# A PEER expert layer at the end of a one-core trunk step: rows of the second stream gathered as 64 tokens with two picks each, query low parts on GpSimd, four pieces of the choice inside the projection

## The reference, cut to what matters

```python
q = (h @ w_q).reshape(b, l, PEER_HEADS, 2, PEER_KEY_DIM // 2)
s = jnp.einsum('blhpk,hpnk->blhpn', q, sub_keys).astype(jnp.float32)
sv, si = lax.top_k(s, kk)
cand = sv[..., 0, :, None] + sv[..., 1, None, :]
cv, ci = lax.top_k(cand.reshape(b, l, PEER_HEADS, kk * kk), kk)
...
expert = i1 * PEER_N_KEYS + i2
gate = jax.nn.softmax(cv, axis=-1).astype(h.dtype)
...
act = jax.nn.gelu(jnp.einsum('tkd,td->tk', u[ex], hx), approximate=False)
return jnp.einsum('tk,tkd->td', gx * act, v[ex])
```

## Time and profile before

| | |
|---|---|
| median of 3 runs | 3093.76 us (3091.87 to 3102.01) |
| the profiled execution | 3091.47 us, its span 3089.4 us |
| TensorE | busy 75% of the span |
| VectorE | 72% |
| ScalarE | 40% |
| GpSimd | 38% |
| DMA | 866.75 MB, mean 281 GB/s |
| mean granted TensorE clock | 0.862 of full |

### The profile page before, as it was taken

The page is one execution under the profiler, slowest core; times in us unless marked ns, Lnnn a source line. Parts: engine busy times, 40 slices in busy tenths (PEclk is TensorE's granted clock), DMA queues, the critical chain, the costliest instruction groups (busy, mean ns, idle before and its releaser), DMA issues.

```text
span 3089.4 us, 38793 instructions
## 1 busy us (share of the span) xinstructions
PE 2319.5 (75%) x15046; PEld 2046.4 (66%) x15046; DVE 2235.4 (72%) x2892; ACT 1229.6 (40%) x1951; POOL 1168.7 (38%) x793
## 2 busy tenths in 40 slices
PE   6899999999999899999998930000331048999997
PEld 2688889988887798999987930000231047888886
DVE  1344446878888863444545899999999988999985
ACT  1233334545555563433343410000893065444433
POOL 0000000255455530000000022686888846767760
PEclk8899999999999999999999975555555568999998
DMA  9888775544534459876553567999999967999994
GB/s 407 329 305 294 288 289 202 190 141 164 178 137 150 157 199 379 307 265 236 177 204 136 178 282 250 362 421 422 422 421 422 422 225 268 375 376 377 360 365 141
DMA packets 151913, 866.75 MB, mean 281 GB/s; under 512 B 18177, under 2 KB 30481, under 8 KB 74017
## 3 DMA queue, kind: packets, MB, share of 16 engines
q1 hardware_dynamic: 67698, 447.32, 39.4%
q0 software_dynamic: 73872, 406.08, 34.2%
q10 hardware_dynamic: 10160, 10.88, 1.0%
HBM read 836.81 MB, written 27.39 MB: 280 GB/s over the span
## 4 chain that ended last, share of the span: by engine, by line
PE 51%; DVE 15%; POOL 14%; issue 9%; DMA 8%; ACT 2%; DVEq 0%; ACTq 0%; SPq 0%; POOLq 0%
PE bank L1693 30%; POOL u_ring L686 14%; PE bank L2060 7%; PE bank L1679 7%; DMA raw<-in_tiles 4%; DVE w_lo L1109 3%; DMA v_got<-in_v_rest,expert 2%; PE bank L1718 2%; DVE u_ring L1572 2%; DVE peer_g L1600 2%; PE bank L2043 2%; DMA u_ring<-in_peer_u,expert 1%; DVE conv L1223 1%; DVE c_lo L1612 1%; DVE y_w L1281 1%
## 5 line engine op out<-in xcount | busy, mean ns | idle before, releaser
L1109 DVE TENSOR_TENSOR w_lo<-raw,w_hi 128x1024 fp32r<-128x1024 f32 x482 | 638.6, 1339 | 559.9 <-ACT w_hi L729 553.6
L729 ACT ACTIVATE w_hi<-raw 128x1024 fp32r<-128x1024 f32 x482 | 501.1, 1058 | 640.9 <-PE bank L1693 340.3
L686 POOL DMA_INDIRECT u_ring<-in_peer_u,expert x256 | 481.3, 1880 | 409.5 <-PE bank L1693 212.8
L1693 PE MATMUL bank<-h_lo,w_hi 128*128 128x256 f32 x2048 | 592.4, 289 | 14.3 <-DVE h_lo L1155 8.3
L1572 DVE CUSTOM_DVE_ANT_0 u_ring<-u_ring,h_t 128x2048 f32<-128x2048 f32 x256 | 580.2, 2289 | 28.1 <-DMA u_ring<-in_peer_u,expert 26.6
L1693 PE MATMUL bank<-h_hi,w_lo 128*128 128x256 f32 x2048 | 581.5, 284 | 0.0
L1693 PE MATMUL bank<-h_hi,w_hi 128*128 128x256 f32 x2048 | 581.4, 284 | 0.0
L1693 PEld LDWEIGHTS bank<-h_lo,w_hi 128*128 128x128 f32 x2048 | 394.8, 193 | 57.0 <-issue 24.6
L693 POOL DMA_INDIRECT v_got<-in_v_rest,expert x256 | 346.0, 1351 | 183.0 <-DVE peer_g L1600 135.8
L1693 PEld LDWEIGHTS bank<-h_hi,w_lo 128*128 128x128 f32 x2048 | 395.0, 193 | 0.9
L1693 PEld LDWEIGHTS bank<-h_hi,w_hi 128*128 128x128 f32 x2048 | 394.6, 193 | 0.0
(11 more groups left out here) (304 smaller groups left out, 4553.8 us busy)
## 6 DMA issues: line engine op xcount, KB each, us to landing
raw<-in_tiles SPq DMA_DIRECT2D x337, 1024.0 KB, 5.7
v_raw<-in_v_dense SPq DMA_DIRECT2D x128, 660.0 KB, 7.1
s_t<-in_states POOLq DMA_DIRECT2D x8, 512.0 KB, 7.1
y_hi_rows<-y_hi_e POOLq DMA_DIRECT2D x16, 256.0 KB, 2.4
y_lo_rows<-y_lo_e POOLq DMA_DIRECT2D x16, 256.0 KB, 6.2
gate_rows<-gate_buf ACTq DMA_DIRECT2D x8, 512.0 KB, 6.6
y_hi<-y_hi_rows POOLq DMA_DIRECT2D x8, 512.0 KB, 8.3
y_lo<-y_lo_rows POOLq DMA_DIRECT2D x8, 512.0 KB, 4.2
```

What stands on the lines that cost most here:

```text
L686: pool.indirect_dma_start(u_ring[:, U_SLOT[e]], None, a["peer_u"][0], bass.IndirectOffsetOnAxis(ap=expert[:, s, k:k + 1], axis=0)).then_in ...
L729: act.activation(w_hi[:, i % RING], raw[:, slot % SLOTS, (n % 2) * 2 * CH:(n % 2 + 1) * 2 * CH], ACT.Copy) \
L1109: dve.tensor_tensor(w_lo[:, i % RING], raw[:, n // 2 % SLOTS, (n % 2) * 2 * CH:(n % 2 + 1) * 2 * CH], w_hi[:, i % RING].bitcast(F32), ALU. ...
L1693: ins = pe.matmul(spot if x.shape[1] == KT else spot.rearrange("p (s t) -> p s t", s=NS), w[:, col], moving, start=start and k == 0 and m ...
```

## The change

It has four parts.

1. `w_lo` of the 32 halves of the query projection is made by GpSimd (a new semaphore `lo_wq`), no longer by VectorE; both copies of `peer_q` out of PSUM are ScalarE's.
2. The order of the choices is (0,0), (1,0), (0,1), (1,1) in the projection, with nothing in between, then (0,2), (0,3), (1,2), (1,3), with the products of u rows in between.
3. The 128 gathers of stream 1 take other rows: the first 64 bring the picks of tokens 0 to 63 (partitions 0 to 63 hold pick k, 64 to 127 pick k + 64), the last 64 those of tokens 64 to 127. For this SyncE's queue copies `expert`, `gate_t` and `h2_t` into arranged tiles (`expert1`, `gate1`, `h2_late`). After the first 64, their tokens are scattered (16 batches, ScalarE alone makes the one-hot tiles) beside the last 64 gathers.
4. After the last u row, 16 batches are left. ScalarE makes `hot_b` of the even ones, VectorE that of the odd ones (one 128x512 comparison) and all `hot_a`; one v add for every second batch (8), the split of blocks 0 and 1 inside it. The last 64 gathers use a ring of 7 slots; two `v_raw` tiles and two `v_got` tiles lie in slots of that ring, and are filled once those are done with.

```diff
+U_LATE = (16, 17, 18, 12, 13, 14, 15)
...
+CHOICES = [(0, 0), (1, 0), (0, 1), (1, 1), (0, 2), (0, 3), (1, 2), (1, 3)]
...
+            sp.dma_start(h2_late[low], h2_t[high, 1]).then_inc(expert1_in, 16)
+            sp.dma_start(h2_late[high], h2_t[high, 1]).then_inc(expert1_in, 16)
+            for of in (low, high):
+                for to in (low, high):
+                    sp.dma_start(expert1[to, of], expert[of, 1, to]).then_inc(expert1_in, 16)
+            sp.wait_ge(expert1_in, 16 * 6)
+            sp.dma_start(h2_t[high, 1], h2_t[low, 1]).then_inc(gate1_in, 16)
...
             for i in range(N_KEYS):
+                if 0 < i < TABLE:
+                    sp.wait_ge(u_used, max(U_DEAD[17], U_DEAD[18]) + 1)
...
+            for i in range(WQ_NO, len(SPLIT)):
+                n = SPLIT[i]
+                pool.wait_ge(hi_done, i + 1)
+                pool.wait_ge(split_used, SPLIT[i - RING] + 1)
+                pool.tensor_tensor(w_lo[:, i % RING], raw[:, n // 2 % SLOTS, (n % 2) * 2 * CH:(n % 2 + 1) * 2 * CH],
+                                   w_hi[:, i % RING].bitcast(F32), ALU.subtract).then_inc(lo_wq, 1)
...
-            for j in range(4):
-                advance_to(min(FIRST["wq", j] + HALVES + LEAD + 3, N_HALVES + LEAD))
-                limit = min(FIRST["wq", j] + 2 * HALVES + LEAD, N_HALVES + LEAD)
-                choose(0, j, lambda: next_half(limit))
+            while at_half[0] < N_HALVES + LEAD:
+                advance()
+            for s, j in CHOICES[0:4]:
+                choose(s, j, lambda: None)
...
+            one_hot(0, 0)
+            for b in range(BATCHES):
+                if b + 1 < BATCHES:
+                    one_hot(0, b + 1)
+                scatter_copy(0, b)
+                if b == BATCHES - 5:
+                    gelu_of_half(0)
...
+            for b in range(HALF_B, BATCHES):
+                if b % 2 and b + 1 < BATCHES:
+                    one_hot(1, b + 1)
+                scatter_copy(1, b)
+                if b in (HALF_B + 6, HALF_B + 10):
+                    dense_hi((b - HALF_B - 6) // 4)
```

More of the change, by code:

```diff
@@ L46 @@
 BATCHES = P // BATCH
+HALF_T = P // 2
+HALF_B = BATCHES // 2
 NEG = -1.0e30
@@ L126 @@
 U_SLOT, U_TURN, U_LAST = ring_slots()
+U_DEAD = {n: max(e for e in range(NS * SEL) if U_SLOT[e] == n) for n in U_LATE}
 def accumulators():
@@ L433, in program @@
         x2_saved = sem("x2_saved")
-        u_in = [sem(f"u_in{n}") for n in range(2 * U_RING)]
+        u_in = [sem(f"u_in{n}") for n in range(2 * U_RING + 3)]
+        expert1_in = sem("expert1_in")
+        gate1_in = sem("gate1_in")
         u_used = sem("u_used")
@@ L1102, in split @@
             def split(n):
-                if n not in SPLIT_NO:
+                if n not in SPLIT_NO or SPLIT_NO[n] >= WQ_NO:
                     return
@@ L1570, in expert_act @@
                 dve.wait_ge(u_in[U_SLOT[e]], 16 * U_TURN[e] + 16)
-                u = u_ring[:, U_SLOT[e]]
-                dve.tensor_tensor_reduce(out=u, in0=u, in1=h2_t[:, s], scale=1.0, scalar=0.0,
-                                         op0=ALU.mult, op1=ALU.add, accum_out=act_p[:, s, k:k + 1]).then_inc(u_used, 1)
-            def coefficients(s):
-                dve.wait_ge(gelu_done, s + 1)
-                dve.tensor_tensor(coef_p[:, s], act_p[:, s], gate_t[:, s], ALU.mult).then_inc(coef_ready, 1)
+                u = u_ring[U_SLOT[e]]
@@ new lines, in expert_act, with coefficients @@
+                h = h2_t[:, s]
+                if e == SEL:
+                    dve.wait_ge(gate1_in, 16 * 5)
+                if e >= SEL + HALF_T:
+                    h = h2_late[:]
+                dve.tensor_tensor_reduce(out=u, in0=u, in1=h, scale=1.0, scalar=0.0,
+                                         op0=ALU.mult, op1=ALU.add, accum_out=act_p[:, s, k:k + 1]).then_inc(u_used, 1)
+            def coefficients():
+                dve.wait_ge(gelu_done, 1)
+                dve.tensor_tensor(coef_p[:, 0], act_p[:, 0], gate_t[:, 0], ALU.mult).then_inc(coef_ready, 1)
@@ L1619, in take @@
                 taken[0] += 1
-            for j in range(4):
-                choose(1, j, take)
+            for s, j in CHOICES[4:]:
+                choose(s, j, take)
             normalise(0)
             normalise(1)
+            dve.sem_inc(gate_max, 1)
             for e in range(taken[0], SEL):
                 expert_act(e)
-            coefficients(0)
+            coefficients()
             for k in range(SEL):
+                if k == HALF_T + 13:
+                    half_coefficients(0)
                 expert_act(SEL + k)
-            coefficients(1)
-            for i in range(2):
-                dense_lo(i)
-            for b in range(BATCHES):
+            half_coefficients(1)
+            e = 0
+            for b in range(HALF_B, BATCHES):
                 one_hots(b)
-                expert_add(b)
-            e = BATCHES
+                if b % 2 == 0:
+                    expert_add(e)
+                    e += 1
+                if b in (HALF_B + 7, HALF_B + 11):
+                    dense_lo((b - HALF_B - 7) // 4)
             for i in range(N_KEYS):
@@ L2047, in _ @@
             pe.wait_ge(score_in, 4)
-            for s in range(NS):
-                turn_picks(s)
-                for b in range(BATCHES):
-                    scatter(s, b)
+            turn_picks()
+            turn_keys()
+            for b in range(BATCHES):
+                scatter(0, b)
+            turn_coef(0)
+            for b in range(HALF_B):
+                scatter(1, b)
+            turn_coef(1)
+            turn_back()
+            for b in range(HALF_B, BATCHES):
+                scatter(1, b)
+            pe.wait_ge(pick_ready, 5)
             pe.wait_ge(scat_copied, NS * BATCHES)
```

223 lines of the change are left out of this document (146 added, 77 removed).

## The result

The changed kernel takes 3067.4 us (median of 4 runs, 3064.08 to 3069.75), the kernel before 3094.49 us beside it. The ratio is 0.991, with a 95% interval of 0.9896 to 0.9924: faster by 27 us, clear of the noise though under 1%, where 41 to 44 us were forecast, and 1.4 us outside the forecast range (3036 to 3066). A repetition (the fifth experiment) gave 3065.0 us, 0.9903 [0.9885, 0.992]. One of the ten runs of e1 took 10333.66 us and is left out of its ratio.

The account below looks back on a forecast made before the run. Bounds: TensorE in the projection, VectorE then DMA in the gathers; in the scatter ScalarE was busy 77 of 82 us. Terms -8 + 3.8 + 0 - 39.9 + 3.4 = -40.7 us from 3091.47 gave 3050.8, predicted 3050, range 3036 to 3066.

Parts of the forecast that it names:

- What bounds, and the scatter: Stream 1's scatter: first half hides beside gathers with 41 us over; stage after last row 42.7 against 82.6 us, -39.9.
- 4.3 us a pair: After the last u row: each of 8 pairs of scatter batches was taken at 4.3 us, 34.4 in all.
- 1.3 us a split: After the last u row: two splits of a v block inside the chain, 2 x 1.3 us.
- Low parts on GpSimd, and the four choices: Query projection: subtractions on GpSimd cost 0; choices slowed 18 us by waiting, first product at 1813 us, gain 8 us.
- The copies of `h2_t` ... at 417 GB/s cost 3.8 us: Gather stage: three 64x2048 copies, 1.57 MB, add 3.8 us of DMA time in a saturated stretch; bounds 0 and 3.8.
- Two move to the last five rows; same bytes, so 0: Gather stage: two of three first `v_raw` loads move to the last five rows, at cost 0.
- The v side: 124 blocks carry adds, not 112: 12 x (3.88 - 3.60) = +3.4 us, bounds 0 and 6.
- The rivals: Five alternatives: late choices (0.17), everything hides (0.14), late pairs no faster (0.05), GpSimd binds projection (0.04), first-half scatter late (0.02).
- The late choices: Rival: GpSimd and VectorE hold each other up, first product at 1821 us or later; 3058 to 3065 us, chance 0.17.
- the ring of 7: Last 64 gathers: one slot less (7 for 8) leaves 15 us for a gather to land; cost taken as 0.

Follow-up runs that it names:

- the fifth experiment: The changed kernel run again unaltered, beside three variants on one chip: 3065.03 us, 0.9903.
- e1: The kernel before with only GpSimd's low parts and the new order of choices (parts 1 and 2): 3088.85 us against 3094.3, 0.9982.
- e12: e6 with VectorE's split of v blocks 0 and 1 one batch later in its queue: 3051.87 us, 0.9851.
- e2: The changed kernel with GpSimd subtracting only 8 of 1024 columns of each projection half, waits kept: 3055.7 us, 0.9884.
- e3: The changed kernel with the three copies of `h2_t` issued when `h2_t` is complete, not after the last choice: 3056.11 us, 0.9875.
- e6: The changed kernel with the edits of e3 and e4 together: 3051.24 us, 0.9863.
- e7: As e6, but the copies of `h2_t` wait for the fifth choice: 3051.3 us, 0.9869.
- e8: The changed kernel with one extra 128-partition copy of `h2_t` (1.05 MB) ahead of the others: 3066.7 us in one run.
- e11: The changed kernel with the eight 16 KB copies of `expert` and `gate_t` made twice: 3068.01 us in one run.
- e4: The changed kernel with the loads of v blocks 1 and 2 issued after the last product of a u row: 3062.13 us, 0.9895.
- e10: The changed kernel without the gathers of v rows 5 to 255, all 256 adds kept: 3047.83 us in one run.

## Why the prediction was off

**What bounds, and the scatter: right.** The early half of the scatter hid with 43 us to spare (41 worked out), and the stage after the last row is 42.0 us (42.7). Inside it the terms were off, 3.68 for 4.3 us a pair and 2.9 and 3.4 for 1.3 us a split; that the sum fits within 0.8 us is luck. The split is dear because it is a chain over two engines: ScalarE's 1.29 us, then VectorE's 1.53, then the hot tile queued behind. e12 shows it.

**Low parts on GpSimd, and the four choices: mechanism right, size near.** TensorE stayed the bound of the projection (102.73 of 103 us, e1), and the two engines held each other up by 20 us, forecast 18; with the 0.8 us from the last choice to the product and chance, the first product came 3.9 to 6.7 us earlier, not 8. e2 shows that the mutual waiting is all of it. The Trainium skill, "SBUF — State Buffer", section "Who interferes with whom", also says that the reduction never contends and that a cast can; the trace agrees in both, with 0.69 us always and once 2.32 us for a 128x32 cast (0.18 alone).

**"The copies of `h2_t` ... at 417 GB/s cost 3.8 us": the step that failed.** I priced bytes at the rate of 128-partition transfers; the term of +3.8 us, called an upper end, measured +7.6. The three copies touch 64 partitions each, and while they run the rate is 250 GB/s at full DMA share. Product 121 lost 7.6 us although two v loads (3.2 us) had left the stretch, so the gross cost is near 11 us by my estimate; the 7.8 us that the engines lost from 1952.5 to 1980 us and the 3.8 of the copies' own bytes make 11.6. e3 takes 7.1 us back by moving them. The early copies are not free either: from product 1 to 253 e3, e6 and e7 still lose 1.4 to 2.0 us, with the two v loads gone, where e1, without copies and with all its v loads, loses 0.4. e8 and e11 exclude copies within SBUF as such, and small pieces. That 64 partitions are the reason is what these two leave, and the two rows under e8 show it in the rate: 0.52 against 0.86 MB in 2.5 us. The crossing from one half of the partitions to the other wasn't tested apart from it. The Trainium skill, "SBUF — State Buffer", section "Door 1: The DMA port swizzle (why `[64,N]` ≈ `[32,N]`)", says that partitions 0 to 63 reach only half of the DMA's ports, and so do 64 to 127. By this rule 1.57 MB cost 7.5 us at half of 417 GB/s, an estimate from that page's rule and this trace's rate. The 7.1 us that e3 takes back lie nearer to it than to my 3.8; the gross estimate of 11 us lies over both, and no run tells what the copies take from what the gathers beside them lose.

**"Two move to the last five rows; same bytes, so 0": right as a sum, wrong as a place.** The 3.2 us left the stretch near 1955 us and came back as 3.3 us of waits in the last three rows. But in the new place they need not have been paid, with idle DMA engines (share 0.39) right behind; e4 has them there for nothing.

**The v side: wrong by 5.8 us, half understood.** I had 12 x 0.28 us for 12 more blocks with adds. e10 shows that VectorE's 3.75 us, not TensorE's 3.60, is the floor of such a block and that the gathers of v rows cost time on top. With this v side eight of the eleven kernels took 516.5 to 520.2 us, 1 to 5 more than the 515.4 of the kernel before, around the 3.4 that I had forecast. But e1, whose v side is that of the kernel before, took 518.5, so these few microseconds are not told apart from chance. The changed kernel, its repetition and e11 took 524.6, 524.0 and 522.5, with the same code behind the first matmul. Waits of VectorE in this part, changed kernel, then e3:

```profile
DVE peer_g L1690 <- DMA v_got<-in_v_rest,expert: 22.9, 28, 2.5
```

```profile
DVE peer_g L1690 <- DMA v_got<-in_v_rest,expert: 17.1, 23, 2.5
```

Five more waits for a v row, 5.8 us. Why these kernels have them and the others not stays open.

**The rivals.** The late choices (3058 to 3065 us) were the nearest case by number, but not by cause: in the changed kernel the choices cost 3 us of the 18 that were missing in the profiled execution, the copies and v loads 7, the v side 6, the mark 2, and 1 lies between products 121 and 253, where e6 and e7 lose 1.5 and 2.1; whether the ring of 7 has a part in it no run shows. The scatter gave 1 back. No forecast case had the copies as its mechanism, though their bound of 3.8 us was called an upper end.

## What to carry to other kernels

Price a DMA by its bytes and by the partitions that it touches, and look for a full DMA share at a low rate in the trace. Issue a copy when its source is complete, and not with the last thing that its queue waits for: in this kernel the same three copies cost 6 to 7 us more at 1951 us than at 1815 or 1850 us; a prefetch into a saturated end is better held back until the engines fall idle. Compare two traces by the n-th turn of the stage's own loop from a mark at its entry: this gave the loss from product 1 to 121 alike to 0.01 us in two executions, though product 1 itself lay 1.2 us apart and single runs of one kernel differ by several.

## What was not expected of the hardware

Three copies of 64x2048 float32 within SBUF held the DMA engines at 250 GB/s and full share for some 15 us, while one of 128x2048 added 2.7 us for 1.05 MB. The v side, with one and the same code, took from 516.5 to 524.6 us; the one kernel that was profiled twice gave 524.6 and 524.0, which hints at the kernel and not the execution, but two profiles don't show it.
